# Value products in two column halves, and a re-ordered second attention, in a two-block transformer kernel

## The reference

```python
# first block: a window of 128 keys back, so one or two key blocks of 128
scores = jnp.einsum("bnqkgd,bnjkd->bnkgqj", qb, kw).astype(jnp.float32) * scale
p = jnp.exp(scores - m[..., None])
denom = jnp.sum(p, axis=-1) + jnp.exp(sink - m)
probs = (p / denom[..., None]).astype(v.dtype)
out = jnp.einsum("bnkgqj,bnjkd->bnqkgd", probs, vw)
y_attn = sliding_window_attention_with_sinks(...) * jax.nn.silu(g_attn)

# second block: causal, one to four key blocks, keys picked by an index score
_, sel = lax.top_k(score, topk)          # the 128 best keys of each position
logits = jnp.einsum('bqgrd,bqkgd->bqgrk', qg, kg).astype(jnp.float32) * scale
p = jax.nn.softmax(logits, axis=-1).astype(vg.dtype)
o = jnp.einsum('bqgrk,bqkgd->bqgrd', p, vg)
```

## Time and profile before

| what | us |
|---|---|
| median of 3 runs | 1800.95 |
| lowest and highest of them | 1800.46, 1800.96 |
| the profiled execution | 1798.12 |
| its span (first to last instruction) | 1796.3 |
| TensorE busy, share of the span | 95% |
| VectorE, ScalarE busy | 58%, 40% |
| first attention, about | 163 to 412 of the span |
| second attention, about | 717 to 827 of the span |

### The profile page before, as it was taken

How to read it: one execution, slowest core, us unless ns; L and a number is a source line. 1 busy time by engine, 2 the same in 40 slices (tenths; PEclk the granted TensorE clock), 3 DMA queues, 4 the chain that set the end, 5 groups by cost and what they waited for, 6 DMA issues and landing times.

```text
span 1796.3 us, 22583 instructions
## 1 busy us (share of the span) xinstructions
PE 1703.9 (95%) x7512; PEld 1325.6 (74%) x7512; DVE 1042.9 (58%) x2080; ACT 722.9 (40%) x1378; POOL 63.1 (4%) x43
## 2 busy tenths in 40 slices
PE   5999999999998997898899999999999899999999
PEld 4777667777886765346788888887888788888887
DVE  7788666666455688873655554367444543333334
ACT  4363766663343232774433322324323333332322
POOL 0020000000000045000000000000000000000000
PEclk9999999999998998799999999999999999999999
DMA  6343334444231111001255555243323223323333
GB/s 234 131 162 96 118 128 163 143 145 141 93 94 59 59 58 49 1 1 47 65 210 200 194 190 171 94 169 125 94 95 105 83 82 96 102 94 96 104 94 106
DMA packets 55815, 201.68 MB, mean 112 GB/s; under 512 B 6193, under 2 KB 6321, under 8 KB 55601
## 3 DMA queue, kind: packets, MB, share of 16 engines
q1 hardware_dynamic: 55728, 200.57, 33.5%
HBM read 198.44 MB, written 2.10 MB: 112 GB/s over the span
## 4 chain that ended last, share of the span: by engine, by line
PE 82%; DVE 10%; ACT 5%; issue 2%; DMA 0%; POOL 0%; DVEq 0%; ACTq 0%; SPq 0%; POOLq 0%
PE bank L449 25%; PE bank L451 24%; PE bank L450 24%; PE bank L585 2%; ACT SB L992 1%; DVE SB L1576 1%; PE bank L574 1%; DVE W_lo L1359 1%; PE bank L555 1%; PE bank L491 1%; ACT PT L1006 1%; PE bank L492 1%; DVE G L1429 1%; PE bank L506 1%; PE bank L675 1%
## 5 line engine op out<-in xcount | busy, mean ns | idle before, releaser
L449 PE MATMUL bank<-H_hi,W_hi 128*128 128x512 f32 x1368 | 553.2, 404 | 10.6 <-DVE H_lo L1421 4.8
L450 PE MATMUL bank<-H_lo,W_hi 128*128 128x512 f32 x1368 | 535.3, 391 | 0.0
L451 PE MATMUL bank<-H_hi,W_lo 128*128 128x512 f32 x1368 | 535.0, 391 | 0.0
L1359 DVE TENSOR_TENSOR W_lo<-RAW,W_hi 128x512 fp32r<-128x512 f32 x538 | 351.9, 693 | 193.0 <-ACT W_hi L865 177.5
L865 ACT ACTIVATE W_hi<-RAW 128x512 fp32r<-128x512 f32 x538 | 316.9, 625 | 252.2 <-PE bank L451 215.0
L449 PEld LDWEIGHTS bank<-H_hi,W_hi 128*128 128x128 f32 x1368 | 257.8, 188 | 95.8 <-issue 32.7
L450 PEld LDWEIGHTS bank<-H_lo,W_hi 128*128 128x128 f32 x1368 | 258.1, 189 | 57.5 <-issue 6.9
L451 PEld LDWEIGHTS bank<-H_hi,W_lo 128*128 128x128 f32 x1368 | 258.1, 189 | 55.1
L451 PE MATMUL bank<-A_hi,W_lo 128*128 128x512 f32 x352 | 137.0, 389 | 0.0
L450 PE MATMUL bank<-A_lo,W_hi 128*128 128x512 f32 x352 | 136.9, 389 | 0.0
L449 PE MATMUL bank<-A_hi,W_hi 128*128 128x512 f32 x352 | 136.9, 389 | 0.0
(11 more groups left out here) (258 smaller groups left out, 1996.0 us busy)
## 6 DMA issues: line engine op xcount, KB each, us to landing
RAW<-weights SPq DMA_DIRECT2D x269, 512.0 KB, 3.6
AW<-ada SPq DMA_DIRECT2D x100, 512.0 KB, 3.5
X<-x_t SPq DMA_DIRECT2D x4, 512.0 KB, 6.9
y_t<-X SPq DMA_DIRECT2D x8, 256.0 KB, 2.0
LW<-lru_w SPq DMA_DIRECT2D x1, 1024.0 KB, 13.1
CROW<-crow SPq DMA_DIRECT2D x1, 512.0 KB, 11.1
ROPE<-rope SPq DMA_DIRECT2D x1, 512.0 KB, 13.9
CS<-constants SPq DMA_DIRECT2D x1, 386.5 KB, 9.1
```

The costliest lines, as they stand in the source:

```text
L449: pe.matmul(dst, wh, ch(hi, k), start=(k == 0), stop=False)
L450: pe.matmul(dst, wh, ch(lo, k), start=False, stop=False)
L451: mm = pe.matmul(dst, wl, ch(hi, k), start=False, stop=(k == chunks - 1))
L1359: dve.tensor_tensor(W_lo[:, w], RAW[:, c:c + HALF], W_hi[:, w], ALU.subtract).then_inc(lo_done, 1)
```

## The change

The value product of a key block is issued as two matmuls of 256 columns, one for the even heads into partitions 0 to 63 of bank 6, one for the odd heads into partitions 64 to 127, each with the same 64 columns of values as weights. Bank 6 then holds the heads in the form that `YT` had; `heads_out` is gone, and VectorE and ScalarE read bank 6 (in the first attention VectorE multiplies by the gate from bank 6 into `YT`). The transposes put the four heads into another order in their bank. `pv(s)` now waits for the reader of bank 6: `yy_done` (`y_gate(s - 1)`) in the first attention, `y_lo_done` (`y_out(s - 1)`) in the second.

In the second attention all four heads of `qk(s + 2)` stand behind `turn_probs(s)`; `exps(s + 1)` stands ahead of `heads_hi(s - 1)` and `probs_out(s)`; and VectorE's order is `y_out(s - 2)`, `normalise(s)`, all of `score(s + 2)`, `minus_max(s + 2)`, `select`.

```diff
             def pv(s):
                 g, n, keys = STEPS[s]
                 PT = PT1 if s < 16 else PT2
-                if s:
-                    pe.wait_ge(yt_out, s)
+                if 0 < s <= 16:
+                    pe.wait_ge(yy_done, s)
+                elif s > 16:
+                    pe.wait_ge(y_lo_done, s)
                 for c, kb in enumerate(keys):
                     pe.wait_ge(pt_out, PT_COUNT[s] + c + 1)
-                    mm = pe.matmul(ps[6][0:HD, :], V[:, at_col:at_col + HD],
-                                   ch(PT, c), start=(c == 0), stop=(c == len(keys) - 1))
+                    for odd in range(2):
+                        mm = pe.matmul(ps[6][odd * HD:(odd + 1) * HD, 0:2 * P], V[:, at_col:at_col + HD],
+                                       PT[:, c * S + odd * 2 * P:c * S + (odd + 1) * 2 * P],
+                                       start=(c == 0), stop=(c == len(keys) - 1))
                 mm.then_inc(pv_mm, 1)
...
             for s in range(16, 32):
-                if s < 31:
-                    qk(s + 1, (3,))
-                if s < 30:
-                    qk(s + 2, (0,))
                 turn_probs(s)
                 if s < 30:
-                    qk(s + 2, (1, 2))
+                    qk(s + 2)
                 pv(s)
...
-            def heads_out(s):
...
             exps(16)
             for s in range(16, 32):
+                if s < 31:
+                    exps(s + 1)
                 if s > 16:
-                    heads_out(s - 1)
                     heads_hi(s - 1)
                 probs_out(s)
-                if s < 31:
-                    exps(s + 1)
...
             for s in range(16, 32):
+                if s > 17:
+                    y_out(s - 2)
                 normalise(s)
-                if s < 31:
-                    score(s + 1, 3)
-                    if s + 1 == 19:
+                if s < 30:
+                    for h in range(4):
+                        score(s + 2, h)
+                    if s + 2 == 19:
                         query_roots(2)
-                    minus_max(s + 1)
+                    minus_max(s + 2)
                 if s < 26:
                     select(ROUNDS_S[s - 16])
-                if s < 30:
-                    for h in range(3):
-                        score(s + 2, h)
-                if s > 16:
-                    y_out(s - 1)
+            y_out(30)
             y_out(31)
```

More of the change, by code:

```diff
@@ L855, in _ @@
         def _(act):
-            chain = Tally(act_chain)
             def split_hi(tile, halves=range(2), fn=ACT.Copy):
@@ L1025, in heads_hi @@
                     act.wait_ge(yy_done, s + 1)
+                    heads = YT[:, :]
                 else:
-                    act.wait_ge(yt_out, s + 1)
-                    act.wait_ge(act_chain, chain.n)
-                act.copy(y_region(YA_hi, s), YT[:, :].rearrange("p (k t) -> p k t", k=2)).then_inc(y_hi_done, 1)
+                    act.wait_ge(pv_mm, s + 1)
+                    heads = ps[6][:, 0:2 * P]
+                act.copy(y_region(YA_hi, s), heads.rearrange("p (k t) -> p k t", k=2)).then_inc(y_hi_done, 1)
             fn_count = [0]
@@ L1089, in _ @@
                     fill_hi(s, 0)
-            heads_out(15)
             heads_hi(15)
@@ L1214, in _ @@
             for s in range(16, 32):
+                if s < 31:
+                    exps(s + 1)
                 if s > 16:
-                    heads_out(s - 1)
                     heads_hi(s - 1)
                 probs_out(s)
-                if s < 31:
-                    exps(s + 1)
-            heads_out(31)
             heads_hi(31)
@@ L1583, in y_gate @@
             def y_gate(s):
-                dve.wait_ge(yt_out, s + 1)
+                dve.wait_ge(pv_mm, s + 1)
                 yt = YT[:, :].rearrange("p (k t) -> p k t", k=2)
+                if s:
+                    dve.wait_ge(y_lo_done, s)
                 if s % 4 == 0:
                     dve.wait_ge(ga_done, GA_NEED[s // 4])
-                dve.tensor_tensor(yt, yt, y_region(GA, s), ALU.mult).then_inc(yy_done, 1)
+                heads = ps[6][:, 0:2 * P].rearrange("p (k t) -> p k t", k=2)
+                dve.tensor_tensor(yt, heads, y_region(GA, s), ALU.mult).then_inc(yy_done, 1)
             def y_out(s):
-                yt = YT[:, :].rearrange("p (k t) -> p k t", k=2)
+                heads = (YT[:, :] if s < 16 else ps[6][:, 0:2 * P]).rearrange("p (k t) -> p k t", k=2)
                 dve.wait_ge(y_hi_done, s + 1)
-                dve.tensor_tensor(y_region(YA_lo if s < 16 else YA2_lo, s), yt, y_region(YA_hi, s), ALU.subtract).then_inc(y_lo_done, 1)
+                dve.tensor_tensor(y_region(YA_lo if s < 16 else YA2_lo, s), heads, y_region(YA_hi, s),
+                                  ALU.subtract).then_inc(y_lo_done, 1)
             GA_NEED = [2, 4, 6, 8]
@@ L1953, in _ @@
             minus_max(16)
-            for h in range(3):
+            for h in range(4):
                 score(17, h)
+            minus_max(17)
             for s in range(16, 32):
+                if s > 17:
+                    y_out(s - 2)
                 normalise(s)
-                if s < 31:
-                    score(s + 1, 3)
-                    if s + 1 == 19:
+                if s < 30:
+                    for h in range(4):
+                        score(s + 2, h)
+                    if s + 2 == 19:
                         query_roots(2)
-                    minus_max(s + 1)
+                    minus_max(s + 2)
                 if s < 26:
                     select(ROUNDS_S[s - 16])
-                if s < 30:
-                    for h in range(3):
-                        score(s + 2, h)
-                if s > 16:
-                    y_out(s - 1)
+            y_out(30)
             y_out(31)
```

17 lines of the change are left out of this document (5 added, 12 removed).

## The result

The changed kernel takes 1819.7 us (median of 4 runs, 1818.3 to 1821.7), the kernel before 1800.7 us in the runs beside it (1797.9 to 1801.0): a ratio of 1.011, 95% interval 1.0098 to 1.0123, or 19 us more. The profiled execution has a span of 1817.5 us, against 1796.3 us.

What follows compares the result with a forecast made beforehand. TensorE was taken to bound the first attention, chains of waits, partly along VectorE, the second. First attention -10.6, VectorE's loop +11 and clock +12.6 made +13 us on 1796.3; the difference added to the median gave 1814 us, range 1800 to 1834.

Steps and rivals of the forecast that it cites:

- The value products in the first attention: First attention, TensorE: halves overlap, one key block 0.59 us instead of 1.00, two 1.02 instead of 1.87; -10.6 us.
- The step from the key norms: Inference from 16 key-norm matmuls alternating between partition halves in 1.02 us: they run in pairs, so value-product halves would too.
- The loop on VectorE: Second attention: normalising, transposes, first score product, scores and selection come to stand in series on VectorE; +11 us at unchanged clock.
- The price of the low clock: Second attention at 1.2 GHz: about +2.5 us a step with two key blocks, +3.8 with three, +5.3 with four.
- I take half of the eight steps with two and three at the low level: Second attention, clock term for steps 20 to 27: +12.6 us, bounds 0 and +30.
- Steps 28, 29 and the tail: End of second attention, four key blocks: steps 28 and 29 7.95 us each, then a short tail without scores.
- The steps with one key block: Second attention, steps 16 to 19: 5.5, 6.4, 7.0 and 7.0 us, ending at 746.4.
- The clock stays as it was: Rival: clock unchanged despite longer steps, only -10.6 + 11, 1801.5 us; chance 0.20.
- Clock stays low: Rival: the eight steps with two and three key blocks and half of the last four run low, +30, 1832 us; chance 0.13.
- Faster: Rival: VectorE's hole, about 2.2 us in each of steps 20 to 27, closes and the clock stays; 1784 us; chance 0.12.
- In series: Rival: the product halves do not overlap, saving nothing in the first attention; +36, 1837 us; chance 0.05.

Runs made afterwards that it cites:

- first_halves_only: Kernel before with the value products in two column halves only in steps 0 to 15, second attention as it was: 1789.7 us, ratio 0.9947.
- halves_in_series: Kernel before with each value product cut into two of 256 columns, both into the same 64 partitions: 1798.9 us, ratio 0.9995.
- after_early_y_out: Changed kernel with `y_out(s - 1)` directly behind `normalise(s)`: 1814.2 us, ratio 1.0082 to the kernel before.
- dummy_products: Changed kernel with four added matmuls of 256 columns, into an unread bank, behind the score products of steps 16 to 27: 1808.5 us.
- selection_first: Changed kernel with the selection moved back directly behind `normalise(s)`, ahead of the scores of s + 2: 1793.6 us, ratio 0.9968 to the kernel before.
- halves_old_order: Changed kernel with the second attention back in its old order, halves everywhere, `pv(s)` still waiting for `y_out(s - 1)`: 1800.2 us, ratio 1.000 to the kernel before.

## Why the prediction was right, and where a term was too small

1814 us was forecast, within 1800 to 1834, and slower with 0.70; it was 1819.7. Both main mechanisms were there. That the point lies only 6 us low is in part luck. The second attention took 140.5 us, where the sum had 117.5 + 12.6 = 130.1, 10.4 us too little. Of these the earlier start gives back 2.5 us (13.1 where 10.6 were forecast), and another 2.4 us come from adding the 2.8 us between profile and median of the kernel before, where the changed kernel has 0.4 (1819.29 and 1819.7). Term by term:

- **The value products in the first attention: right.** 0.59 and 1.02 us were forecast, 0.58 and 1.01 measured; -10.6 us were forecast and first_halves_only gave -9.9; the first tile behind the first attention starts at 405.56 in the changed kernel and at 415.44 before, 9.9 us earlier too. The step from the key norms, that products to different halves of the partitions overlap, is shown by halves_in_series. The waits that swallow a part of it are there too: 2.08 us instead of 1.02.
- **Some us more ahead of the second attention: not in the sum, and left open.** The changed kernel stood 13.1 us earlier at the first reciprocal, and first_halves_only, whose code is nearly the same up to there, 11.4 us (709.12). What goes beyond the 10 us grew between 430 and 640 us, where the work is that of the kernel before. A part of it is chance: after_early_y_out has the code of the changed kernel up to the first reciprocal and stands there at 711.16, dummy_products at 708.86, the changed kernel at 707.49. These three and first_halves_only are 9.4 to 13.1 us earlier than the kernel before; whether any of what lies beyond 9.9 is more than chance, no run shows.
- **The loop on VectorE: right, +11 us.** All three signs came: idle time ahead of the first score that the score product ends, TensorE waiting for `y_out`, and longer steps. selection_first shows it to be the cause, with 26 us for that one move, the clock's part included. The size is shown for the three steps that dummy_products ran at a granted clock of 1.00, 20 to 22: 0.3 us more than the terms in each.
- **The price of the low clock ("the transposes and products in the loop double"): right for two key blocks.** +2.5 us a step was forecast, and 10.98 - 8.40 = 2.6 us measured in step 21.
- **"I take half of the eight steps with two and three at the low level": right for the eight together, not for where.** The table has the steps by their reciprocals; "forecast" is at unchanged clock.

| steps | forecast | changed kernel | dummy_products |
|---|---|---|---|
| 16 to 19, one key block | 25.9 | 29.4 | 28.5 |
| 20 to 23, two | 32.3 | 41.4 | 34.8 |
| 24 to 27, three | 33.2 | 39.4 | 37.1 |
| 28, 29, four | 15.9 | 18.0 | 16.6 |
| 30 to the next tile | 10.2 | 12.3 | 10.8 |
| sum | 117.5 | 140.5 | 127.8 |

The windows of the changed kernel over steps 20 to 23, 24 to 27, 26 alone and 27 alone:

```profile
736.86:778.28 41.42, 25.78 (x92) 14.46 (x92) 24.36 (x82) 17.51 (x48) 0.00 (x0) 0.62 0.00 0
778.28:817.65 39.37, 28.25 (x124) 15.25 (x124) 22.84 (x73) 17.05 (x41) 0.00 (x0) 0.82 0.00 1
800.07:810.19 10.12, 8.75 (x32) 4.77 (x32) 4.61 (x17) 2.35 (x5) 0.00 (x0) 0.71 0.01 2
810.19:817.65 7.46, 6.08 (x32) 3.04 (x32) 4.61 (x17) 4.99 (x13) 0.00 (x0) 1.00 0.00 0
```

With two levels, 0.62 means that 76% of the time was at the low one, and 0.82 that 36% was: about three of the four steps with two key blocks and one and a half of the four with three, four and a half of the eight. At the forecast prices that is 3.0 x 2.5 + 1.4 x 3.8 = 12.8 us, against 12.6 in the sum. The eight steps lost 9.1 + 6.2 = 15.3 us; the other 2.5 us fit the 0.3 us a step by which dummy_products shows the loop's terms to be short. Among the steps with three, step 26 lost 2.9 us at 0.71 and step 27 0.2 us at 1.00, so the 3.8 us a step were paid by fewer steps; the rows don't show the price to be wrong.
- **Steps 28, 29 and the tail: low clock put at nothing, 4.2 us too short.** The sum had the clock's price for steps with four key blocks (5.3 us) only in its bound. Both rows are 2.1 us over the forecast: step 29 took 9.87 us instead of 7.95 at a granted clock of 0.83, and step 30 had 0.64. dummy_products ran all four steps at 1.00 and was 0.7 and 0.6 us over, so some 2.9 us of the 4.2 are the clock and the rest are terms too short. This is the largest part of the 10.4 us.
- **The steps with one key block: 3.5 us too short.** They were priced at the low level already. For steps 18 and 19 the four scores and the maxima were put at 1.57 us; at 1.2 GHz VectorE also waited for the fourth score product, 0.57 us in step 18 as in 19, and 0.46 us in 16 and 17, 2.1 us in all. That wait stands in no term. The rest is the first score, which came 0.2 to 0.4 us later in each of the four steps than the terms have it. VectorE of the changed kernel:

```profile
726.71 0.42 DVE L1924 CUSTOM_DVE_ANT_0 SB<-bank,BIAS 128x256 f32<-128x256 f32 x1 [0.57 <-PE bank L555]
```

- **The rivals.** "The clock stays as it was" falls with the windows. "Clock stays low" came nearest behind the forecast: at 1820 us the time lies between the two, and the rival's premise held for three quarters of the time in the steps with two key blocks. Its +30 is also summed too low: 4 x 2.5 + 4 x 3.8 + 2 x 5.3 is 35.8 us, which puts the rival at 1837 us and not 1832. "Faster" needed the hole to close, and it did not: 4.39 us of it. "In series" falls with the timeline.
- **What I had not priced apart** is the place of `y_out`. The prediction named the wait of `pv(s)` for it inside the loop, and that loop ends the same way. But halves_old_order shows that this wait costs the whole gain of the halves even in the old order, and I had expected 1789 us for it. I had taken it that with the selection in its old place the loop is open; it is not while TensorE waits for the last operation of a VectorE step.

Still open: how much of the 23.0 us beyond the forecast at unchanged clock (140.5 - 117.5) the clock alone made. dummy_products gave back 12.7 us of it (140.5 - 127.8) with its clock still at 0.82 from 760 to 785, and with more work, so the clock made at least about 12.7 us.

The granted clock swung between its two levels: 0.71, 0.50, 0.65, 0.66, 0.81, 0.82, 0.71 and 1.00 in steps 20 to 27, with waits of 2.6 to 4.2 us ahead of the value products of steps 20 to 24. This agrees with the rule that the prediction cited (the Trainium skill, "TensorE: Matmul & The Clock Gate", section "A second HAM failure mode: psum-queue depth-cycling"): short idle spells between groups of matmuls make the clock swing.

## What to carry to other kernels

When a buffer gets a new reader, look where that reader stands in its engine's order: an operation of 0.42 us behind a selection of 3 us cost 12 us here, and moving it was free. Look also at what the moved operation waits for itself: in the other order the same move cost 6 us, until ScalarE's cast was moved too. Fill the hole between "A has given TensorE its input" and "A needs TensorE's output" with work that depends on neither; putting the dependent read first opens the hole, 26 us here. And price a loop with TensorE in it at both levels of the clock, for every step of the stage: half of the eight middle steps at the low level was about right here, and the largest shortfall was in the four steps behind them, which the sum left at the high one.

## What was unexpected of the hardware

- Adding 48 matmuls of 256 columns to the critical engine made the kernel 11 us faster, as the granted clock rose from 0.50 to 0.79 (726 to 740) and from 0.59 to 1.00 (740 to 760). Ten matmuls of 512 columns ahead of the stage did not do this: TensorE had 1.00 from 690 to 706 with them, then waited 3.39 us, and had 0.57 from 706 to 726, against 0.50 without them.
- Two products of 256 columns into the two halves of the partitions, from the same 64 columns of weights, took little more than half the time of the same two into one half: 0.58 and 1.01 us for the four matmuls of a key block in the trace.
